# Strassen's scheme in the down projections of three of four MLP passes, with POOL forming the low parts of all fourteen weight units of each

## The reference

```python
D_MODEL = 1024
SEQ = 512
DEPTH = 2
D_FF = 4 * D_MODEL
...
    for layer in range(DEPTH):
...
        h = h + squared_relu_mlp(rmsnorm(h, mlp_norm[layer]), w_up[layer], w_down[layer])
    return rmsnorm(h, final_norm)
```

## Time and profile before

| what | value |
| --- | --- |
| median of 3 runs | 1301.35 us (1301.01 to 1302.15) |
| profiled execution, its own time | 1299.8 us |
| its span | 1298.0 us |
| mean granted TensorE clock | 0.989 of full speed |
| PE busy share | 97% |
| DVE, ACT, POOL busy share | 57%, 47%, 46% |
| DMA | 109.18 MB, mean 84 GB/s |

### The profile page before, as it was taken

The page is one execution under the profiler, slowest core; times in us unless marked ns, Lnnn a source line. Parts: engine busy times, 40 slices in busy tenths (PEclk is TensorE's granted clock), DMA queues, the critical chain, the costliest instruction groups (busy, mean ns, idle before and its releaser), DMA issues.

```text
span 1298.0 us, 19296 instructions
## 1 busy us (share of the span) xinstructions
PE 1255.2 (97%) x7549; PEld 1057.7 (81%) x7549; DVE 739.0 (57%) x1099; ACT 616.1 (47%) x990; POOL 594.9 (46%) x689
## 2 busy tenths in 40 slices
PE   6999978999999999999999999999999999999997
PEld 5777756788998988988777778888888898998986
DVE  4438665572562734743789975476554373562743
ACT  5335674463362542734582634753554263361641
POOL 4653224756256083373445543312656426265080
PEclk9999998999999999999999999999999999999999
DMA  9322101336153251422222321000334335152311
GB/s 283 95 74 71 61 17 33 101 94 174 45 151 87 82 148 32 131 68 63 71 61 65 97 66 49 2 2 1 98 102 111 112 116 143 47 142 74 97 34 65
DMA packets 173482, 109.18 MB, mean 84 GB/s; under 512 B 4570, under 2 KB 170704, under 8 KB 173392
## 3 DMA queue, kind: packets, MB, share of 16 engines
q1 hardware_dynamic: 172976, 107.88, 29.2%
q0 software_dynamic: 416, 0.07, 0.0%
HBM read 105.83 MB, written 2.10 MB: 83 GB/s over the span
## 4 chain that ended last, share of the span: by engine, by line
PE 86%; DVE 8%; ACT 3%; issue 2%; DMA 1%; SPq 0%; DVEq 0%; ACTq 0%
PE ps L1251 9%; PE ps L1252 9%; PE ps L1253 9%; PE ps L1217 6%; PE ps L1216 6%; PE ps L1215 6%; PE ps L1120 6%; PE ps L1121 5%; PE ps L1122 5%; PE ps L1107 3%; PE ps L1229 2%; PE ps L1230 2%; PE ps L1231 2%; PE ps L1594 1%; PE ps L1170 1%
## 5 line engine op out<-in xcount | busy, mean ns | idle before, releaser
L998 POOL TENSOR_TENSOR w_lo<-raw_w,w_hi 128x256 fp32r<-128x256 f32 x248 | 213.0, 890 | 266.8 <-ACT w_hi L1747 266.8
L2460 DVE TENSOR_TENSOR h<-h,ps 128x512 f32<-128x512 f32 x64 | 44.0, 687 | 211.2 <-PE ps L1253 211.2
L1120 PE MATMUL ps<-hn_hi,w_hi 128*128 128x512 f32 x368 | 153.1, 416 | 2.5 <-POOL w_lo L998 2.4
L1121 PE MATMUL ps<-hn_lo,w_hi 128*128 128x512 f32 x368 | 146.6, 398 | 0.0
L1122 PE MATMUL ps<-hn_hi,w_lo 128*128 128x512 f32 x368 | 146.6, 398 | 0.0
L1066 POOL TENSOR_TENSOR wx_lo<-raw_w,wx_hi 128x256 fp32r<-128x256 f32 x128 | 98.1, 800 | 40.1 <-ACT wx_hi L1813 40.1
L1813 ACT ACTIVATE wx_hi<-raw_w 128x1024 fp32r<-128x1024 f32 x62 | 65.4, 1054 | 104.1 <-PE ps L1253 91.6
L1066 POOL TENSOR_TENSOR wx_lo<-y_mix,wx_hi 128x256 fp32r<-128x256 f32 x64 | 51.8, 842 | 137.4 <-ACT wx_hi L1813 137.4
L1813 ACT ACTIVATE w_hi<-raw_w 128x1024 fp32r<-128x1024 f32 x54 | 57.0, 1055 | 113.1 <-PE ps L1253 102.9
L1066 POOL TENSOR_TENSOR w_lo<-raw_w,w_hi 128x256 fp32r<-128x256 f32 x120 | 90.0, 783 | 42.8 <-ACT w_hi L1813 42.8
L1251 PE MATMUL ps<-hid_hi,w_hi 128*128 128x512 f32 x256 | 101.1, 395 | 0.0
(11 more groups left out here) (477 smaller groups left out, 3347.8 us busy)
## 6 DMA issues: line engine op xcount, KB each, us to landing
raw_w<-in_w_up SPq DMA_DIRECT2D x40, 512.0 KB, 4.2
raw_w<-in_w_down SPq DMA_DIRECT2D x40, 512.0 KB, 4.1
raw_w<-in_o_w_in SPq DMA_DIRECT2D x27, 512.0 KB, 3.7
y_mix<-in_w_up SPq DMA_DIRECT2D x24, 512.0 KB, 4.6
y_mix<-in_w_down SPq DMA_DIRECT2D x24, 512.0 KB, 4.5
raw_w<-in_e_w_in SPq DMA_DIRECT2D x19, 512.0 KB, 3.7
raw_w<-in_e_w_out SPq DMA_DIRECT2D x8, 512.0 KB, 3.5
raw_w<-in_o_w_out SPq DMA_DIRECT2D x8, 512.0 KB, 3.7
```

Source lines behind the costliest of these rows:

```text
L998: nc.gpsimd.tensor_tensor(w_lo[:, n % CUT, ks], raw_w[:, n % RING, ks], w_hi[:, n % CUT, ks].bitcast(F32), ALU.subtract).then_inc(w_cut, 1)
L1120: mm(o, a_hi, b_hi, start=(k == 0), stop=False)
L1121: mm(o, a_hi, b_lo, start=False, stop=False)
```

## The change

In passes 0, 1 and 2 of both layers the down projection also becomes a scheme of seven products in two halves: fourteen units with 24 matmuls of 256 columns, where eight with 24 of 512 stood. Pass 3 stays plain. In detail:

- Weights: the quarters are A, B, C, E. Three operands are sums (A + C, C + E, and G = A + C + E + B in steps; m6 reads A + C + E, m4 reads G whole). No engine adds them: SP loads a quarter, and POOL issues from its own queue a DMA with an accumulate operation that adds the next quarter in place (`add_load`), ten per pass.
- Low parts: `low_unit` on POOL makes those of all fourteen units and of up units 12 and 13, each now in two instructions of 128x512.
- Activations: the quarters of the squared relu are kept in fp32 (`kept`); DVE forms four differences and sums of them (`form`, d3, d1, d2, d4, 128x1024 each), ACT rounds seven operands (`operand_high`, 128x1024) and DVE makes their low parts (`operand_low`, 128x1024, L2691 and L2688 of the changed file). For these passes the eight roundings and eight subtractions that made `hid_hi` and `hid_lo` during the up projection are gone.
- Output: 16 additions or subtractions of PSUM into quarters of `h` (`fold`, 128x2x256, L2722 of the changed file) replace eight of 128x512.
- Waits: a product waits for its operand's low part, and for the folds that free its PSUM bank. ACT rounds both halves of a product's weights, then its operand, in the order m5, m6, m3, m7, m4.
- SP loads ten quarters per down projection, eight of them into the places of the up units and two (B0, B1) again after m2; the next pass's up loads follow behind the low parts of m5, m3, m7, m4.

The core of the diff:

```diff
+PRODUCTS = ["m1", "m2", "m5", "m6", "m3", "m7", "m4"]
+DN = [(q, p) for q in PRODUCTS for p in range(2)]
...
+DOWN_READS = {"m1": "A", "m2": "B", "m5": "A", "m6": "G", "m3": "B", "m7": "C", "m4": "G"}
...
+FORMED = ["d3", "d1", "d2", "d4"]
+FOLDS = [(f, p) for f in ("a1", "b1", "z5", "x6", "z3") for p in range(2)]
+FOLDS += [("x7", 0), ("y7", 0), ("x7", 1), ("y7", 1), ("v4", 0), ("v4", 1)]
...
 def cut_on_pool(i, u):
+    if u >= ups(i):
+        return True
     return i == 0 or u >= NUP - 2
...
+DOWN_LOADS = [("A0", 0), ("G0", 0), ("B0", 0), ("C0", 0), ("A1", 0), ("G1", 0), ("B1", 0), ("C1", 0), ("B0", 1), ("B1", 1)]
...
+ADDED = {"A": ["C"], "C": ["E"], "G": ["C", "E", "B"]}
...
-            _counts[_on] += PARTS if _on else 1
-            CUT_COUNT.append((_on, _counts[_on]))
+            _parts = 1 if not _on else 2 if in_halves(_i, _u) else PARTS
+            _counts[_on] += _parts
+            CUT_COUNT.append((_on, _counts[_on], _parts))
...
                 def low_unit(i, u):
-                    raw_, (hi_, lo_) = place(layer, place_name(i, u)), cut_buffers(layer, i, u)
+                    raw_, (hi_, lo_) = place(layer, place_no(i, u)), cut_buffers(layer, i, u)
                     pool.wait_ge(u_high, unit(layer, i, u) + 1)
-                    for q in range(PARTS):
-                        c = slice(q * 256, (q + 1) * 256)
+                    parts = CUT_COUNT[unit(layer, i, u)][2]
+                    w = KT * SW // parts
+                    for q in range(parts):
+                        c = slice(q * w, (q + 1) * w)
                         nc.gpsimd.tensor_tensor(lo_[:, c], raw_[:, c], hi_[:, c].bitcast(F32), ALU.subtract
                                                 ).then_inc(u_cut_pool, 1)
...
+                def add_load(i, name, n):
+
+                    at = down_at(i, name)
+                    if name[0] == "A":
+                        unit_cut(pool, layer, i, dnu(i, "m1", int(name[1])))
+                    elif n == 0:
+                        is_loaded(pool, at, layer, i, "down", name, 0)
+                    elif n == 1:
+                        is_added(pool, layer, i, name, 0)
+                    else:
+                        unit_cut(pool, layer, i, dnu(i, "m6", int(name[1])))
+                    pool.dma_start(quarters_of(place(layer, at)),
+                                   down_quarter(layer, i, ADDED[name[0]][n], int(name[1])), accum_op=ALU.add
+                                   ).then_inc(u_added[at], 16)
...
+                for i in range(4):
+                    if i == 0:
+                        for u in range(6):
+                            low_unit(0, u)
+                        add_load(0, "G0", 0)
+                        low_unit(0, 6)
+                        low_unit(0, 7)
+                        add_load(0, "G0", 1)
+                    else:
+                        for p in range(2):
+                            sum_first(i, p)
+                            sum_third(i, p)
+                        if i < 3:
+                            add_load(i, "G0", 0)
+                            add_load(i, "C0", 0)
+                            add_load(i, "G0", 1)
+                        low_unit(i, NUP - 2)
+                        low_unit(i, NUP - 1)
+                    if i == 3:
+                        for j in range(KT):
+                            low_unit(3, NUP + j)
+                        continue
+                    low_unit(i, dnu(i, "m1", 0))
+                    add_load(i, "A0", 0)
+                    low_unit(i, dnu(i, "m1", 1))
+                    add_load(i, "A1", 0)
+                    if i == 0:
+                        add_load(i, "C0", 0)
+                    add_load(i, "G1", 0)
+                    low_unit(i, dnu(i, "m2", 0))
+                    if i:
+                        add_load(i, "C1", 0)
+                    low_unit(i, dnu(i, "m2", 1))
+                    low_unit(i, dnu(i, "m5", 0))
+                    add_load(i, "G1", 1)
+                    low_unit(i, dnu(i, "m5", 1))
+                    low_unit(i, dnu(i, "m6", 0))
+                    low_unit(i, dnu(i, "m6", 1))
+                    if i == 0:
+                        add_load(i, "C1", 0)
+                    add_load(i, "G0", 2)
+                    add_load(i, "G1", 2)
+                    for q in ("m3", "m7", "m4"):
+                        low_unit(i, dnu(i, q, 0))
+                        low_unit(i, dnu(i, q, 1))
...
+                def down_product(i, q, p):
+                    folded_first = {"m6": "a1", "m3": "z5", "m7": "x6", "m4": "b1"}
+                    if q == "m1":
+                        pe.wait_ge(relued, hid_turn(layer, i, ("c22", p)) if i else hid_turn(layer, 0, 6 + p))
+                    elif q in folded_first:
+                        pe.wait_ge(folded, down_turn(FOLDS, layer, i, (folded_first[q], p)))
+                    elif q == "m2" and layer + i:
+                        pe.wait_ge(folded, 16 * (3 * layer + i))
+                    x_hi, x_lo = (v.rearrange("p a t -> p (a t)") for v in operand(layer, i, q))
+
+                    def before(k):
+                        if k == 0 and p == 0:
+                            pe.wait_ge(op_low, 7 * (3 * layer + i) + PRODUCTS.index(q) + 1)
+
+                    bank_ = (D_BANK if q in ("m2", "m4") else BANK_OF[q]) + p
+                    product(ps[:, bank_, :], i, dnu(i, q, p),
+                            lambda k: (x_hi[:, k * HT:(k + 1) * HT], x_lo[:, k * HT:(k + 1) * HT]),
+                            q in ("m1", "m2", "m5", "m4"), before)
...
+                def operand_high(i, q):
+
+                    n = 7 * (3 * layer + i) + PRODUCTS.index(q)
+                    c = {"m1": "c11", "m2": "c12", "m5": "c21", "m6": "c21", "m3": "c12", "m7": "c11", "m4": "c22"}[q]
+                    if q in ("m1", "m2"):
+                        f = {"m1": 3, "m2": 7}[q]
+                        act.wait_ge(hid_square, hid_turn(layer, i, (c, 1)) if i else hid_turn(layer, 0, f))
+                    elif q != "m4":
+                        made = {"m5": "d1", "m6": "d2", "m3": "d4", "m7": "d3"}[q]
+                        act.wait_ge(formed, down_turn(FORMED, layer, i, made))
+                    if PRODUCTS.index(q) >= 3:
+
+                        unit_done(act, layer, i, dnu(i, PRODUCTS[PRODUCTS.index(q) - 3], 1))
+                    A(operand(layer, i, q)[0], kept[c].rearrange("p (a b) t -> p a (b t)", b=2), ACT.Copy,
+                      scale=-1.0 if q == "m6" else 1.0).then_inc(op_high, 1)
...
+                        first = ups(i)
+                        for n, q in ((3, None), (4, "m5"), (6, "m6"), (8, "m3"), (10, "m7"), (12, "m4")):
+                            if n > 3:
+                                high_unit(layer, i, first + n)
+                                high_unit(layer, i, first + n + 1)
+                            elif i == 0:
+                                high_unit(layer, 0, first + 3)
+                                third_high()
+                            if q:
+                                operand_high(i, q)
                         for u in range(4):
                             high_unit(layer, i + 1, u)
...
+                def operand_low(i, q):
+
+                    n = 7 * (3 * layer + i) + PRODUCTS.index(q)
+                    c = {"m1": "c11", "m2": "c12", "m5": "c21", "m6": "c21", "m3": "c12", "m7": "c11", "m4": "c22"}[q]
+                    src = kept[c].rearrange("p (a b) t -> p a (b t)", b=2)
+                    hi_, lo_ = operand(layer, i, q)
+                    dve.wait_ge(op_high, n + 1)
...
+                    else:
+                        V.tensor_tensor(lo_, src, hi_.bitcast(F32), ALU.subtract).then_inc(op_low, 1)
...
+                def fold(i, f, p):
+
+                    q, rows, cols, op = {"a1": ("m1", 0, 0, ALU.add), "b1": ("m2", 0, 0, ALU.add),
+                                         "z5": ("m5", 1, 1, ALU.add), "x6": ("m6", 0, 1, ALU.subtract),
+                                         "z3": ("m3", 0, 1, ALU.add), "x7": ("m7", 1, 1, ALU.subtract),
+                                         "y7": ("m7", 1, 0, ALU.add), "v4": ("m4", 1, 0, ALU.add)}[f]
+                    unit_done(dve, layer, i, dnu(i, q, p))
...
+                    bank_ = (D_BANK if q in ("m2", "m4") else BANK_OF[q]) + p
+                    hq = quarter_of_h(rows, cols, p)
+                    V.tensor_tensor(hq, hq, ps[:, bank_, :].rearrange("p (a t) -> p a t", t=HT), op).then_inc(folded, 1)
...
+                    form(i, "d3")
+                    form(i, "d1")
+                    fold(i, "a1", 0)
+                    operand_low(i, "m5")
+                    if i == 0:
+                        third_low()
+                    fold(i, "a1", 1)
+                    form(i, "d2")
+                    fold(i, "b1", 0)
+                    operand_low(i, "m6")
+                    fold(i, "b1", 1)
+                    form(i, "d4")
```

(34 more changed lines are left out.)

678 lines of the change are left out of this document (388 added, 290 removed).

## The result

The changed kernel takes 1395.72 us (median of 4 runs, 1390.32 to 1397.24), the one before 1301.18 on the same chip: a ratio of 1.0718, with a 95% interval of 1.0688 to 1.0747. It is 94 us slower, on the side that was forecast, but three times as far as the 30 us of the sum, and just above the range's end of 1395.

The account below looks back on a forecast made before the run. PE bounded the kernel before; POOL was to pace the new down projections. 1299.8 + 27.6 (passes 1 and 2) + 1.2 (pass 0) = 1328.6 us, 1330.2 on the median's side; forecast 1331 us, 2% slower, range 1285 to 1395.

Parts of the forecast that it names:

- Taking turns with DVE: Down projections, passes 1 and 2: each form or operand low part costs POOL about 1.0 us; nine count, 9 us.
- its lower bound: Turns on POOL's stretch: none of thirteen costs POOL anything, DVE does all the waiting.
- The last sentence of the prediction: Signs of being wrong, among them PE waiting mostly for DVE's operand low parts, making operands the bound, not weights.
- Costs of nothing: Down projections: ACT's 26 us and DVE's 29 us plus turns hide under PE and POOL, but for the m6 chain.
- G1's chain: Passes 1 and 2: two additions, landing 7 us each, then roundings and low part; PE starts m6 near 26 us.
- the clock: TensorE after the wait for m6: may lose 4.0 us each time, 2.8 under POOL; counted nothing, at most 16 us.
- the addition at 389.43: Earlier trace: DVE's 0.69 us addition of PSUM to h, read as falling in POOL's undisturbed 2.83 us unit.
- POOL sets the end: Passes 1 and 2: POOL's low parts end at 49.9 us, the down projection at 51.3; PE alone at 48.5.
- PE's gain: Six down projections, if nothing else moved: 39.4 us instead of 44.4 each, 29.9 us saved in all.
- The "room" on the DMA engines: SP's queue: two more loads and ten more DMAs a pass fit, at a DMA share of 0.35.
- Rival C: Additions in memory land late, at 12 us: 1366 us, at 15 us 1396; decides from about 9.5; chance 0.19.
- Rival B: POOL keeps up, m6 starts before 21.9 us: faster, 1277 to 1298 us; chance 0.15.

Follow-up runs that it names:

- e2: The changed kernel without POOL's accumulating DMAs, POOL only signalling in their place (additions left out, so it computes something else): 1313.01 us, ratio to before 1.0027.
- e6: The changed kernel with POOL waiting, before each low part instruction of the halved units, for its own instruction before to end: 1382.56 us, ratio to before 1.0634.
- e1: The changed kernel with POOL's low parts of the new down units in four instructions of 128x256 instead of two of 128x512: 1425.51 us.
- e4: The changed kernel with DVE instead of POOL making the low parts of six of the fourteen units of each new down projection: 1362.34 us.
- e3: The changed kernel with five waits on POOL per down projection for DVE's forms and operand low parts: 1381.64 us, ratio to before 1.0580.
- e9: The changed kernel with seven units' low parts on DVE, G1's additions issued earlier, and POOL waiting for its own previous instruction: 1335.14 us.

## Why the prediction was wrong, and where it was right

- **The failed step is "Taking turns with DVE".** It priced one turn at 1.0 us for POOL and 0.4 to 0.8 for DVE, from the earlier trace rows, and its lower bound, DVE doing all the waiting, as a gain. There POOL's units came without DMA issues among them, and DVE got in at the next boundary. Behind DMA issues POOL pays nothing, and DVE waits out the run: 9.1 us for an operand low part, 12.5 for two forms. DVE stands in front of PE, by the operand low parts: 79.6 us of waits, most of them by this. The last sentence of the prediction named this sign; no rival had a price for it, and "Costs of nothing" hid DVE's turns under PE and POOL. e2 (no DMAs) and e6 (POOL waiting for itself) each removed it.
- **It is not the whole miss.** With the turns cured and nothing else (e6), the time is still 1382.56, 51 us above the forecast: G1's chain and the clock, below, then take the room.
- One reading in that step was off, without harm: the addition at 389.43 fell between POOL's units, which ended at 389.31 and began again at 390.57. The one at 392.23 falls inside an undisturbed unit (390.57, 2.85 us), so additions of PSUM cost POOL nothing, as counted.
- The Trainium skill, page "SBUF — State Buffer", section "Who interferes with whom", says that issue order, not the shape, decides who blocks; by its section "Summary: rules for kernel authors" the second to issue, DVE with two SBUF inputs or a GpSimd instruction that reads SBUF, blocks until the first finishes. e1 agrees that the shape is not what decides. The rest falls short of what the trace shows: the wait of 9.1 us at 427.85 was for a whole run, and for POOL instructions that began after DVE's.
- **So "POOL sets the end" was wrong**: PE's waits for POOL came to 3.3 us, and with six units fewer (e4) it was still 1362 us.
- **The clock was counted as nothing**, since POOL's pace would hide it, with at most 16 us. Two long gaps a down projection, each followed by a unit of 4.2 to 5.2 instead of 2.8 us, cost some 26, and PE's busy time was 31 above that at the full clock.
- **Right in size**: PE's gain of 29.9 (336 matmuls at 0.117), a unit at 2.54 us (2.53 forecast), an issue at 1.29 (1.2), a landing at 8.0 (7). The fit of the Trainium skill (page "DMA: Bandwidth & Descriptors", section "Anatomy of one DMA — SWDGE (gpsimd) path"), 3.2 us by estimate, is below both the copies' 5.4 and the accumulating 8.0.
- **Right in mechanism, hidden in the changed kernel**: the chain of G1 ahead of m6. It showed, with 6.3 to 6.8 us a down projection in passes 1 and 2, once the lock-out was cured (e3, e6), and went when the additions were issued earlier (e9). The "room" on the DMA engines, from a share of 0.35, was less than thought: with 0.68 to 0.80 over the new down projections, single landings took up to 10.5 us in pass 1.
- Rival C, as it was put, was not the cause: landing at 8.0 at the median lies below the 9.5 from which it decides, and e6, with landings at 7.8, has no long wait at m5 and m3. Rival B's condition was met in part: POOL kept up nearly, but PE began m6 30.8 us after the start, where B needs less than 21.9.
- That 1395.72 lies so close to the range's end is luck: the range was put together from POOL's terms and late landings, with no term for PE's waits for DVE.

What stays open: why narrower instructions made it worse (e1), and by what a DMA issue ahead of a run of POOL lets the whole run go before DVE.

## What to carry to other kernels

When two engines take turns at a resource, price both sides: one may lose nothing while the other waits for its whole run, so ask which of them stands in front of the bound engine. A stretch in which a sharing engine did only one kind of work says little of one in which it also issues DMAs. Where one stall is removed, look for the one behind it: here three (DVE's turn, a landing, the clock after gaps) overlapped, and single cures that keep the additions gave some 10 to 33 us of the 94.
